# Modulation sums loaded by a queue of their own, and four left-hand sides moved in by halves

## The reference, cut to what matters

```python
mod = jnp.dot(silu(c), ada_w) + ada_b                 # 12 pieces of 512 columns
sh1, sc1, g1, sh2, sc2, g2 = jnp.split(mod, 6, axis=-1)
h = modulate(rms_norm(x, norm1_g), sh1, sc1)
z = h @ w_in + b_in                                   # mlstm, attention, and the two gates ga, gb
merged = sigmoid(ga) * (ym @ p_mlstm) + sigmoid(gb) * (ya @ p_moba)
x = x + g1 * (merged @ w_out)
h = modulate(rms_norm(x, norm2_g), sh2, sc2)          # feed-forward norm
x = x + g2 * ((silu(h @ w_gate) * (h @ w_up)) @ w_down)
x = rms_norm(x, normf_g)
# second block
k, v = split(rmsnorm(mem, mem_norm) @ wkv)            # memory keys and values
x = x + short_conv_pool_mixer(rmsnorm(x, mix_norm))   # even norm, e_* stages
x = x + memory_cross_attn(rmsnorm(x, xattn_norm), k, v, wq, wo)   # cross norm, x_q
x = x + peer_ffn(rmsnorm(x, peer_norm))               # gathers 128 rows of (u, v) per token
# then the odd mixer, cross attention, peer_ffn again, and a last norm
```

## Time and profile before

| | us |
|---|---|
| median of 3 runs (2345.34 to 2348.28) | 2345.96 |
| the profiled execution, its own time | 2342.3 |
| its span, first to last instruction | 2340.3 |
| TensorE busy in the span | 2049.8 |
| VectorE busy | 1509.5 |
| ScalarE busy | 766.8 |
| GpSimd busy | 937.8 |

### The profile page before, as it was taken

The page is one execution under the profiler, slowest core; times in us unless marked ns, Lnnn a source line. Parts: engine busy times, 40 slices in busy tenths (PEclk is TensorE's granted clock), DMA queues, the critical chain, the costliest instruction groups (busy, mean ns, idle before and its releaser), DMA issues.

```text
span 2340.3 us, 25020 instructions
## 1 busy us (share of the span) xinstructions
PE 2049.8 (88%) x8364; PEld 1270.3 (54%) x8364; DVE 1509.5 (64%) x3764; ACT 766.8 (33%) x1771; POOL 937.8 (40%) x674
## 2 busy tenths in 40 slices
PE   8988999999999899998778988878999978777776
PEld 4854479987866556543335645534565536333322
DVE  5766532128312668897678676768787677877755
ACT  2321234344222233332333333233434232333332
POOL 2710158788530334444433333232323233344542
PEclk9998999999999999999999998999999989899999
DMA  8535455565442999999999999999999999999997
GB/s 316 213 117 193 173 209 194 171 213 193 148 153 72 359 423 416 413 409 411 424 420 418 405 411 420 419 421 379 421 398 399 381 421 367 403 420 424 414 425 299
DMA packets 139760, 777.33 MB, mean 332 GB/s; under 512 B 15512, under 2 KB 17688, under 8 KB 73072
## 3 DMA queue, kind: packets, MB, share of 16 engines
q0 software_dynamic: 75792, 547.25, 56.6%
q1 hardware_dynamic: 63696, 228.44, 26.4%
q10 hardware_dynamic: 144, 0.05, 0.0%
HBM read 774.62 MB, written 1.06 MB: 331 GB/s over the span
## 4 chain that ended last, share of the span: by engine, by line
PE 46%; DMA 25%; DVE 21%; ACT 4%; issue 2%; POOL 1%; DVEq 0%; SPq 0%; ACTq 0%; POOLq 0%
PE banks L920 14%; PE banks L828 14%; DMA rows_c<-in_uv,p_eid 10%; DMA rows_b<-in_uv,p_eid 7%; PE banks L957 6%; DMA W<-in_weights 6%; PE banks L1166 2%; PE banks L995 2%; DVE rows_b L2440 2%; DVE rows_c L2440 2%; DVE arena L1983 2%; PE banks L1394 2%; DVE arena L2440 1%; ACT arena L1590 1%; PE banks L1130 1%
## 5 line engine op out<-in xcount | busy, mean ns | idle before, releaser
L724 POOL TENSOR_TENSOR W_lo<-W,W_hi 128x1024 fp32r<-128x1024 f32 x141 | 348.4, 2480 | 231.3 <-ACT W_hi L1537 212.3
L920 PE MATMUL banks<-arena 128*128 128x512 f32 x712 | 350.0, 629 | 85.3 <-ACT arena L1599 84.9
L775 POOL DMA_INDIRECT arena<-in_uv,p_eid x192 | 219.1, 1141 | 494.3 <-PE banks L920 396.4
L920 PE MATMUL banks<-rows_b,arena 128*128 128x512 f32 x668 | 325.8, 627 | 57.2 <-ACT arena L1599 57.2
L775 POOL DMA_INDIRECT rows_b<-in_uv,p_eid x192 | 214.9, 1119 | 300.6 <-PE banks L920 229.7
L1588 ACT ACTIVATE arena<-arena 128x2 f32<-128x2 f32 x256 | 52.0, 203 | 814.7 <-DVE arena L1989 809.6
L2440 DVE SCALAR_TENSOR_TENSOR arena<-arena,H 128x1024 f32<-128x1024 f32 x192 | 232.9, 1225 | 99.8 <-DMA arena<-in_uv,p_eid 96.5
L2440 DVE SCALAR_TENSOR_TENSOR rows_b<-rows_b,H 128x1024 f32<-128x1024 f32 x192 | 232.4, 1224 | 99.2 <-DMA rows_b<-in_uv,p_eid 97.5
L920 PEld LDWEIGHTS banks<-arena 128*128 128x128 f32 x712 | 134.2, 199 | 262.3 <-issue 141.5
L920 PE MATMUL banks<-rows_c,arena 128*128 128x512 f32 x460 | 224.7, 631 | 48.5 <-ACT arena L1599 48.5
L920 PEld LDWEIGHTS banks<-rows_b,arena 128*128 128x128 f32 x668 | 129.1, 199 | 230.0 <-issue 145.6
(11 more groups left out here) (311 smaller groups left out, 3079.2 us busy)
## 6 DMA issues: line engine op xcount, KB each, us to landing
W<-in_weights SPq DMA_DIRECT2D x408, 512.0 KB
gain<-in_rows SPq DMA_DIRECT2D x7, 512.0 KB, 12.5
gain<-in_rows POOLq DMA_DIRECT2D x6, 512.0 KB, 5.2
arena<-in_keys SPq DMA_DIRECT2D x3, 1024.0 KB
arena<-in_uv,p_eid POOLq DMA_INDIRECT x192
rows_b<-in_uv,p_eid POOLq DMA_INDIRECT x192
arena<-in_rows POOLq DMA_DIRECT2D x1, 2048.0 KB, 15.2
rows_c<-in_uv,p_eid POOLq DMA_INDIRECT x128
```

The source lines that it names most:

```text
L724: po.tensor_tensor(W_lo[:, slot, :], W[:, (PARTS * n + part) % RAW_RING, :], W_hi[:, slot, :].bitcast(F32), ALU.subtract).then_inc(S_("lo_ ...
L775: po.indirect_dma_start(rows[slot], None, io[f"uv{l}"], bass.IndirectOffsetOnAxis(ap=p_eid[:, t, j:j + 1], axis=0))\
L920: mm = pe.matmul(banks[:, plan.bank(f"p_v{c}", b), :], diag[:, m % DIAGS, :], rows[slot][:, D + b * BLK:D + (b + 1) * BLK], start=j == 0, ...
```

## The change

1. The six sum tiles leave the SP list and become an input of their own, `sums`. POOL loads their 24 parts into three slots `sum_in`, which lie on the memory of `W_hi`. A load waits until the part three before it has been summed. The first ten loads stand in POOL's program behind the last subtraction of the z products and ahead of the load of `m_row`, the other fourteen ahead of `load_gain(2)`. ScalarE's copies for `w_out` now wait for all 24 sums. `PARTS_IN_M`/`PARTS_IN_A` spread the sums otherwise; four parts come after `y_T`. `y_T` goes ahead of `ada4` to `ada6` on PE and DVE.
2. `T1`, `T4` and `T5` are transposed by halves of the blocks: g = 0 of both token blocks, then g = 1. For `T1` and `T5` DVE makes the norm by halves of 512 columns (`norm_halves`, signals `h_half` and `h_ready`). The product that follows waits for the two transposed banks of a half at parts 0 and 2 rather than for all four. Filler: `ff_g0` 2 to 1, `x_q` 1 to none, `e_pv` 2 to none, `x_k0` 6 to 1.
3. The split memory side is waited for by halves at `x_k0`, and ScalarE makes the first two copies of `x_k0`'s weights between the two halves of the memory.
4. `x_v0` becomes `x_v0a` and `x_v0b`. `T4` stands between them in the plan, and in PE's program between parts 1 and 2 of `x_v0b`.
5. One subtraction of `ff_u0` goes ahead of POOL's wait for the feed-forward norm.

The core of the diff:

```diff
-PARTS_IN_M = [2, 2, 2, 4]
-PARTS_IN_A = {1: 2, 3: 2, 5: 2, 7: 4}
+PARTS_IN_M = [2, 2, 3, 3]
+PARTS_IN_A = {1: 2, 2: 1, 3: 2, 4: 1, 5: 2, 6: 1, 7: 1}
...
     p.add("a_pv", NT)
+    p.add("y_T", 4)
     for i in SUMMED[:3]:
         p.add(f"ada{i}")
-    p.add("y_T", 4)
...
     p.add("x_k0", 4)
-    p.add("x_v0", 4, "scalar")
+    p.add("x_v0a", 2, "scalar")
     p.add("T4", 4)
+    p.add("x_v0b", 2, "scalar")
...
-    t += [("gate1", 0), ("sum4", 0), ("gate3", 0), ("sum5", 0), ("sum6", 0), ("gate5", 0), ("sum7", 0), ("gate7", 0)]
-    t += [("sum8", 0), ("sum9", 0), ("merge0", 3), ("merge1", 3)]
+    t += [("gate1", 0), ("gate3", 0), ("gate5", 0), ("gate7", 0), ("merge0", 3), ("merge1", 3)]
...
+            def load_sums(first, end):
+                for q in range(first, end):
+                    i, part = q // PARTS, q % PARTS
+                    if q >= SPLIT_RING:
+                        po.wait_ge(S_("ada_summed"), 2 * PARTS + q - SPLIT_RING + 1)
+                    po.dma_start(sum_in[:, q % SPLIT_RING, :], io["sums"][i][:, part * PW:(part + 1) * PW])\
+                        .then_inc(S_(f"sum_landed{q % SPLIT_RING}"), 16)
+
+            po.wait_ge(pe_filled, plan.mark("z_n", 9))
+            load_sums(0, sum(PARTS_IN_M))
             po.wait_ge(S_("m_row_free"), 1)
...
+            load_sums(sum(PARTS_IN_M), PARTS * len(SUMMED))
             load_gain(2)
...
+            low("ff_u0", 0, 0, 1)
             po.wait_ge(S_("h_ready"), 2 * NT)
-            low("ff_u0")
+            low("ff_u0", 0, 1)
...
+            def halves_T(n, wait):
+                for g in range(2):
+                    for t in range(NT):
+                        wait(g, t)
+                        bank = claim(f"T{n}", 2 * g + t)
+                        for j in range(4):
+                            mm = pe.transpose(bank[:, j * P:(j + 1) * P], H[:, t, (4 * g + j) * P:(4 * g + j + 1) * P], ident)
+                        mm.then_inc(pe_filled, 1)
...
-            norm_T(1)
-            busy("ff_g0", 2)
-            after(pe, "T1", 3)
+            halves_T(1, half_or_all(1, 0))
+            busy("ff_g0", 1)
...
-            busy("x_k0", 6)
-            pe.wait_ge(S_("mem_split"), 2)
-            transposed("x_k0", 2)
-            natural("x_v0", 2)
-            norm_T(4)
-            busy("e_pv", 2)
-            after(pe, "T4", 3)
-            natural("e_pv", 1)
+            busy("x_k0", 1)
+            transposed("x_k0", 2, ready=lambda g: pe.wait_ge(S_("mem_split"), g + 1))
+            natural("x_v0a", 1)
+            fills = [("x_v0b", t, [(slice(0, BLK), slice(0, BLK), cols_at(t * P, P), False)]) for t in range(NT)]
+            product(tile_no["x_v0b"], fills, None, 0)
+            product(tile_no["x_v0b"], fills, None, 1)
+            halves_T(4, lambda g, t: pe.wait_ge(S_("h_ready"), NT * 4 + t + 1))
+            product(tile_no["x_v0b"], fills, None, 2)
+            product(tile_no["x_v0b"], fills, None, 3)
+            natural("e_pv", 1, ready=halves_turned(4))
...
-                norm_T(5)
-                busy("x_q", 1)
-                after(pe, "T5", 3)
-                transposed("x_q", 2)
+                halves_T(5, half_or_all(5, NT))
+                transposed("x_q", 2, ready=halves_turned(5))
...
+            act.wait_ge(S_("ada_summed"), PARTS * (2 + len(SUMMED)))
             high("w_out", 0, 3)
...
                 high_S(memT[:, 4 * b:4 * b + 4, :], 4 * b)
-            high("x_k0", 0, 3)
-            high("x_k0", 3)
+                if b == 0:
+                    high("x_k0", 0, 2)
+            high("x_k0", 2)
...
-            high("x_v0", i=1)
-            high("e_pv", 0, 3)
-            high_T("T4")
-            for i in range(4):
-                n, t = i // 2, i % 2
-                take(x_vs[0][:, t, n * BLK:(n + 1) * BLK], "x_v0", i)
+            high("x_v0b", 0, 3)
+            for t in range(NT):
+                take(x_vs[0][:, t, 0:BLK], "x_v0a", t)
+            high("x_v0b", 3)
+            wait_used(act, tile_no["x_v0b"], 1)
+            high_T("T4", end=2)
+            high("e_pv", 0, 2)
+            filled(act, "x_v0b", 1)
+            high_T("T4", first=2)
+            high("e_pv", 2, 3)
+            for t in range(NT):
+                take(x_vs[0][:, t, BLK:2 * BLK], "x_v0b", t)
...
+            def norm_halves(n, src, g, shift=None):
+                v.wait_ge(S_("squares_ready"), NT * (n + 1))
+                rstd(stat(604 + n % 2 * NT, NT), stat(608 + n % 2 * NT, NT), D)
+                for half in range(2):
+                    c = slice(half * BLK, (half + 1) * BLK)
+                    signal = "h_ready" if half else "h_half"
+                    for t in range(NT):
+                        stt(H[:, t, c], src[:, t, c], stat(608 + n % 2 * NT + t, 1), g[:, c], ALU.mult, ALU.mult,
+                            signal if shift is None else None)
+                        if shift is not None:
+                            tt(H[:, t, c], H[:, t, c], shift[:, c], ALU.add, signal)
...
-            sum_parts(2)
             a_units = [(p, t) for p in range(4) for t in range(NT)]
...
-            norm(1, X, mod[:, 4, :], mod[:, 3, :])
+            norm_halves(1, X, mod[:, 4, :], mod[:, 3, :])
...
-            norm(5, X, gain_of(5))
+            norm_halves(5, X, gain_of(5))
```

More of the change, by code:

```diff
@@ L326, in is_split @@
 def is_split(stage, i):
-    return not (stage.startswith(("ada", "sum", "gate", "merge", "p_q")) or "." in stage or
+    return not (stage.startswith(("ada", "gate", "merge", "p_q")) or "." in stage or
                 stage in ("e_out", "x_o", "x_k1", "x_v1"))
@@ L551, in build @@
         for n, (stage, i) in enumerate(tiles):
-            if stage == "ada" or stage.startswith("sum"):
-                before = i if stage == "ada" else 2 + int(stage[3:]) - SUMMED[0]
-                used.append([("ada_summed", PARTS * before + part + 1) for part in range(PARTS)])
+            if stage == "ada":
+                used.append([("ada_summed", PARTS * i + part + 1) for part in range(PARTS)])
                 continue
@@ L710, in _, with low @@
             po.wait_ge(S_("lo_made"), SPLIT_RING)
-            def low(stage, i=None):
+            def low(stage, i=None, begin=0, end=PARTS):
                 first = tile_no[stage]
@@ L756, in _ @@
             low("x_k0")
-            low("x_v0")
+            low("x_v0a")
+            low("x_v0b")
             load_gain(5)
@@ L810, in product @@
                 for part in range(PARTS) if one is None else [one]:
[L811 to L812 removed]
+                    if ready and part % 2 == 0:
+                        ready(part // 2)
                     if act is None:
@@ L1116, in _ @@
                          causal_keys, "a_t7", slot=head_of)
+            transposes("y_T", [lambda t, b=b: Z[:, t, MO + b * P:MO + (b + 1) * P] for b in range(8)],
+                       lambda t: after(pe, "a_pv", 1))
             for i in SUMMED[:3]:
                 over_partitions(i)
-            transposes("y_T", [lambda t, b=b: Z[:, t, MO + b * P:MO + (b + 1) * P] for b in range(8)],
-                       lambda t: after(pe, "a_pv", 1))
             after(pe, "y_T", 3)
@@ L1429, in joint @@
                     after(pe, f"x_t.{t}", 1)
-                    after(pe, "x_v0", 3)
+                    after(pe, "x_v0b", 1)
                     for g in range(2):
@@ L2882, in lay_out @@
     keys = a["peer_keys_2"].transpose(0, 4, 1, 2, 3).reshape(2, P, 16 * NK)
-    return {"weights": weights, "cols": cols, "small": small, "rows": rows, "pos": pos, "rel_bias": a["rel_bias_2"],
+    return {"weights": weights, "sums": np.stack(ada[4:10]), "cols": cols, "small": small, "rows": rows, "pos": pos, "rel_bias": a["rel_bias_2"],
             "x": a["x"], "mem": a["mem_2"], "keys": keys,
```

54 lines of the change are left out of this document (30 added, 24 removed).

## The result

The changed kernel takes **2331.61 us** (median of 4 runs, 2327.48 to 2333.03), the kernel before beside it 2345.89. The ratio is 0.9935, with an interval of [0.9915, 0.9955]: faster by 14.3 us by the medians. The forecast was 2325.8, so sign and place were right and the size was 5.8 too large. The profiled execution took 2333.03 (span 2331.2), 9.3 less than the one of before.

A forecast was written before the change was run, and what follows sets the result against it. The kernel was taken as bound by one chain up to the fixed-length peer layer; -23.1 - 1.8 - 0.4 + 0 + 6.1 - 1.0 = -20.2 from the 2345.96 median gave 2325.8 us, range 2316 to 2337.

The forecast's parts named there:

- The peer layer is a block of nearly fixed length: From slice 18 DMA fetches a fixed number of rows, so chain gains before 770 us count one to one.
- The bank trap: Memory's values: x_v0b gets x_k0's last banks, so PE waits 7.2 us for DVE's take; +6.1, bounds +3 and +9.
- `merge0` -1.8: merge0 follows y_T at once, so its slow start goes: 13.90 us instead of 15.70.
- the cross norm: Scalings by halves let the product start after two splits, 672.9 instead of 673.9: -1.0, between -1.3 and 0.
- The memory's keys: At x_k0, an earlier start against idle and clock loss from less filler: taken as 0, between -1.1 and +1.5.
- the attention stage: Stage with the gates: sums out of the ring end gate waits and clock loss, 91.5 us instead of 114.6, -23.1.
- the feed-forward norm: Norm and T1 by halves, ready at 330.5 instead of 330.87: -0.4, between -0.9 and +0.5.
- threshold of 6.4: Mlstm sums end before PE needs DVE at 175.9 while a part's load L is below 6.4 us; 5.2 assumed.
- loads late: Rival: with sum loads of 9.5 us the mlstm sums end 9.3 later, 2335 us; chance 0.12.
- the clock falls all the same: Rival: other idle still lowers PE's clock; three falls cost the 10.4 us again, 2336 us; chance 0.12.
- the even norm: PE's old x_v0 to e_pv stretch, read from one profile; hiding T4 was meant to give -5.1, forecast +6.1.
- The slower rival: Round trips through three slots stall DVE; loads of 11.3 us cost the whole gain, 17.2 gives 2381; chance 0.05.

The follow-up runs named there:

- the second profile of the changed kernel: The changed kernel run again with no edit, in a later session beside the kernel before: 2331.56 us, ratio 0.9945.
- exchanged banks: The changed kernel with only the plan's bank numbers exchanged, T4 getting 0 to 3 and x_v0b 6 and 7: 2318.41 us, ratio 0.9887.
- the sums alone: The kernel before with only the sums taken out of the ring and y_T moved ahead, no left-hand side by halves: 2329.19 us, ratio 0.9950.
- two slots: The changed kernel with T4's and x_v0b's banks exchanged, and two slots instead of three for the sums' parts: 2333.43 us, ratio 0.9966.
- spread sums: The changed kernel with sum parts 2, 2, 2, 2 behind the mlstm units instead of 2, 2, 3, 3: 2326.57 us, ratio 0.9929.
- the feed-forward norm whole: The changed kernel with T1 and its norm in the old whole form, filler of two: 2330.91 us, ratio 0.9953.
- the other mends: The changed kernel with sums spread, T1 whole and fillers, plus banks exchanged (2317.35 us, 0.9889) or keys taken early and filler before T4 (2319.14 us, 0.9900).
- halves and exchanged banks: The kernel before with only the four left-hand sides by halves and T4's and x_v0b's banks exchanged: 2342.39 us, ratio 0.9989.

## Why the prediction came out as it did

**Right.** The peer layer is a block of nearly fixed length behind one chain: what the landmarks gain at 770 us is what the spans gain, within the 7 us by which that block varies. The bank trap, +6.1 forecast, is +6.3 in the profile of the changed kernel, with the wait, its releaser and the place as named. The wait was 9.56 instead of 7.2, and the low clock cost less. That the sizes agree so closely is luck: the second profile of the changed kernel has +8.2 for the same stretch. `merge0` -1.8 and the cross norm (-1.0, measured -1.2 with its stretch) are right. The memory's keys, forecast at nothing, measure +0.2; inside, 1.3 gained at the start and 1.5 lost to the clock (0.4 in the second profile). The forecast's terms are -20.2 and the landmarks -13.3; the difference of 6.9 is 5.2 in the attention stage and 2.6 at the feed-forward norm, less 0.9 in the rest. The profiled executions differ by 9.3 and the medians by 14.3, so that a miss of only 5.8 is in part luck too.

**Wrong in size: the attention stage.** -23.1 was forecast and -17.9 measured. The step that failed is the one that let the clock loss go completely: it took the loads at 5.2, "the like kind of transfer", and so had them inside the threshold of 6.4. In that stretch their median was 6.4 (6.3 to 6.9 in the six other profiles with three slots and ten loads in the stretch), and the load on which the chain hung took 8.6. DVE was 2.0 late, PE idled 1.65, and the gate behind lost 2.9 and `y_T` 1.5. This is a mild form of the rivals "loads late" and "the clock falls all the same", coupled: the idle stands right ahead of the slow gate. For `y_T` that coupling isn't shown. I had priced L = 7.3 at 2.6, from the sums' end alone, and had left out that a short wait of PE also costs a slow gate. The runs show that the forecast stage exists: 126.1 from score to `w_out` with exchanged banks, where the forecast has 152.1 - 24.9 = 127.2, by the same code in this stage.

**Wrong by a reading of one profile.** The old form of `x_v0` with `T4` was taken at the 31.1 of the one profile; the sums alone gave 35.8 for the same code. I charged the even norm against one execution, which may have been a lucky one. Against the 35.8 the changed kernel's stretch is 1.6 longer in the first profile and 3.5 in the second.

**The slower rival** needed loads of 11.3. The longest that DVE waited for in the mlstm part took 8.6 in the changed kernel and 8.5 with two slots, and no median of this stretch is above 8.0 (spread sums). The Trainium skill's page "SBUF — State Buffer" (SBUF: two separate sides) describes loads from GpSimd that starve while DVE runs certain operations. DVE was busy for 74.36 of the 96.68 us, and the sums' loads were 1.5 us slower than SP's loads of the same size in the mlstm part (6.4 against 4.9), but only 0.2 to 1.0 slower in three other profiles (6.7 against 6.5 with the feed-forward norm whole, 6.6 against 6.0 with the sums alone). That may be this effect or the crowd of one queue; no run separated the two. What it cost is told above, and it is far from a starved queue. The kernel with two slots shows that the rival was real all the same, at another price: one slot less gives back 0.79 of 1.13%.

What stays open: the medians of exchanged banks and of the changed kernel differ by 13 and the landmarks explain 7 by the banks and up to 4 by the clock in the attention stage. Whether the exchange has a share in the latter, 300 us upstream of it, wasn't tried, and nothing in the code says so. The parts of the change don't add up, for a cause that no run shows. The best version is the changed kernel with exchanged banks, at a ratio of 0.9887, 0.6% better than the change as made; with the other mends added (0.9889, 0.9900) it is no different.

## What to carry to other kernels

When work is moved ahead of other work, look up which buffers it is handed and who empties them last: here a plan that deals out banks in order made the second half of a tile wait 9.6 us for an engine it had nothing to do with, and three lines that only renumber banks gave 7 us of that stretch back. Take the price of a load from the stretch in which it counts, not from the median of the kernel, and look at the loads of the chain one by one; where they lie near a threshold, moving work off that stretch (here two of ten sums) made the engine behind it early enough. Don't put filler ahead of a step before its wait is measured in the final version: filler meant for an idle of 3 us in one kernel was itself the delay in the next. Don't add up parts that were measured alone.

## What the runs showed of the hardware

DVE operations on 128x2 elements took 2.28 to 2.32 us instead of 0.16 to 0.17 while POOL subtracted from SBUF in 2.3 to 2.4 us a piece, some with one SBUF input only (the TENSOR_SCALAR at 541.86). How many of the norm's dozen small operations were caught differed from profile to profile, and `down` to `e_pv` took 120.2 and 124.9 with the same code.

The same idle doesn't always cost the same: after 1.09 us of idle `y_T` took 3.44 and 3.50 in the two profiles of the changed kernel (granted clock 0.55 and 0.54) and 1.97 in six others. After 0.75 of idle `a_pv` took 5.57 in twelve profiles, 8.27 with halves and exchanged banks and 8.35 in the second profile of the changed kernel (granted clock 0.64), though PE had been busy there without a gap from 203 to 219, at a granted clock of 1.00. More or longer idles ahead of it don't decide this: `y_T` was fast with the sums alone, where PE had idled 2.8 at 192. The clock was 1.00 over the whole stage with exchanged banks; windows view:
```profile
142.26:232.65 90.39, 87.47 (x317) 48.38 (x316) 73.88 (x141) 26.16 (x57) 11.07 (x21) 1.00 0.65 212
```
